# A transformer kernel's first stage on one core: the memory norm placed behind the third query block, weight residuals placed ahead of long VectorE pieces, tables and rotations spread

## What is computed

```python
mem_n = rms_norm(mem, mem_norm)                  # mem: 256 x 1024
h  = rms_norm(x, mix_norm[0])                    # x: 1024 x 1024
kv = mem_n @ w_mem_kv[l]                         # for both layers: memory keys and values
p  = h @ w_in                                    # 2048 columns
q, k, v, mq = split(p, [1024, 1280, 1536])
q, k = partial_rotary(q, positions), partial_rotary(k, positions)
attn = window_gqa(q, k, v, sinks)                # the next stage
```

## Time and profile before

| | us |
|---|---|
| median of 3 runs | 3354.19 (3350.89 to 3355.37) |
| the profiled execution, its own time | 3352.99 |
| span of its trace | 3351.2 |
| TensorE busy | 3127.3 (93%) |
| VectorE busy | 1694.6 (51%) |
| ScalarE busy | 1110.0 (33%) |
| the attention's first matmul starts at | 296.18 |

### The profile page before, as it was taken

One profiled execution on the slowest core, in us unless ns is written; L12 is line 12 of the kernel. 1 busy time (PEld: TensorE's weight loads), 2 busy tenths in 40 slices (PEclk: granted clock), 3 DMA queues, 4 the chain that ended last, 5 costly groups with the idle time before them and its releaser, 6 DMA issues.

```text
span 3351.2 us, 34636 instructions
## 1 busy us (share of the span) xinstructions
PE 3127.3 (93%) x14248; PEld 2414.6 (72%) x14258; DVE 1694.6 (51%) x2152; ACT 1110.0 (33%) x1726; POOL 130.6 (4%) x100
## 2 busy tenths in 40 slices
PE   7799989999999999999889999999998899997788
PEld 5686557788888888877667788888886686664556
DVE  6545864544444433599644533333335526664455
ACT  4213652311111111488532211111114417775332
POOL 0001530000000000000000000000002200000000
PEclk9899999999999999999899999999999899999889
DMA  3230011121222211211211111111111220001112
GB/s 135 85 95 26 1 57 38 38 82 63 76 70 75 69 51 51 82 41 41 84 55 38 51 44 50 45 47 48 46 49 57 79 91 20 19 26 69 32 45 101
DMA packets 54366, 190.44 MB, mean 57 GB/s; under 512 B 6272, under 2 KB 6656, under 8 KB 54080
## 3 DMA queue, kind: packets, MB, share of 16 engines
q1 hardware_dynamic: 54208, 188.22, 17.1%
HBM read 172.20 MB, written 14.68 MB: 56 GB/s over the span
## 4 chain that ended last, share of the span: by engine, by line
PE 73%; DVE 13%; ACT 10%; issue 3%; POOL 0%; DMA 0%; DVEq 0%; ACTq 0%; SPq 0%; POOLq 0%
PE PS L283 72%; ACT p L138 8%; DVE p L141 5%; DVE p L144 2%; DVE sm L499 1%; PE PS L534 1%; ACT wsp L138 1%; ACT H L138 1%; DVE p L148 1%; DVE p L1149 1%; DVE wsp L141 1%; DVE H L141 1%; ACT L138 1%; DVE p L547 0%; DVE p L149 0%
## 5 line engine op out<-in xcount | busy, mean ns | idle before, releaser
L283 PE MATMUL PS<-H,wsp 128*128 128x512 f32 x6864 | 1639.4, 399 | 107.6 <-DVE p L144 33.4
L283 PEld LDWEIGHTS PS<-H,wsp 128*128 128x128 f32 x6864 | 1309.8, 192 | 423.8 <-issue 58.0
L283 PE MATMUL PS<-p,wsp 128*128 128x512 f32 (+1 forms) x3840 | 895.1, 393 | 30.3 <-DVE p L141 20.7
L283 PEld LDWEIGHTS PS<-p,wsp 128*128 128x128 f32 x3840 | 713.8, 190 | 207.0 <-ACT wsp L138 21.5
L138 ACT ACTIVATE p<-p 128x1024 f32<-128x1024 f32 (+7 forms) x426 | 360.7, 871 | 879.9 <-DVE p L144 706.4
L138 ACT ACTIVATE wsp<-raw 128x1024 fp32r<-128x1024 f32 (+1 forms) x266 | 275.7, 1039 | 744.4 <-PE PS L283 576.7
L141 DVE TENSOR_TENSOR p<-p,PS 128x1024 f32<-128x1024 f32 (+2 forms) x232 | 244.3, 1053 | 498.2 <-PE PS L283 498.2
L141 DVE TENSOR_TENSOR wsp<-raw,wsp 128x1024 fp32r<-128x1024 f32 (+1 forms) x266 | 322.3, 1216 | 160.2 <-ACT wsp L138 154.9
L141 DVE TENSOR_TENSOR p<-PS,p 128x1024 f32<-128x1024 f32 (+1 forms) x114 | 130.7, 1148 | 443.5 <-PE PS L283 419.4
L283 PE MATMUL PS<-p 128*64 128x256 f32 (+9 forms) x1432 | 291.8, 472 | 23.9 <-ACT p L138 10.3
L141 DVE TENSOR_TENSOR p<-p 128x1024 fp32r<-128x1024 f32 (+6 forms) x245 | 243.4, 1000 | 110.0 <-ACT p L138 107.8
(11 more groups left out here) (71 smaller groups left out, 1167.9 us busy)
## 6 DMA issues: line engine op xcount, KB each, us to landing
raw<-in_in_dram SPq DMA_DIRECT2D x70, 512.0 KB, 3.6
raw<-in_dn_dram SPq DMA_DIRECT2D x68, 512.0 KB, 3.5
raw<-in_up_dram SPq DMA_DIRECT2D x64, 512.0 KB, 3.5
raw<-in_out_dram SPq DMA_DIRECT2D x40, 512.0 KB, 3.5
p<-in_ada_dram SPq DMA_DIRECT2D x24, 512.0 KB, 4.5
p<-in_x_dram SPq DMA_DIRECT2D x16, 512.0 KB, 7.5
raw<-in_kv_dram SPq DMA_DIRECT2D x16, 512.0 KB, 3.7
spill_dram<-p SPq DMA_DIRECT2D x16, 512.0 KB, 2.9
```

The lines of the kernel that those rows point to most:

```text
L283: return pe(lambda e: e.matmul(o, l, r, start=start, stop=stop, **kw), *a)
```

## The change

The order of the same work, nothing else:

- The list `order` has the query blocks and the memory blocks in another sequence: blocks 0 to 5 of `in0` first, and one query block between two pairs of memory blocks from then on.
- MR, the memory norm's factor, is made behind `q_block(2)` instead of before the first two evacuations. Its matmuls so take another place in the turn of PSUM pairs.
- `ahead()` is new: it calls `split` for the next three blocks at once, and it stands before each long VectorE piece.
- The tables: angles and cosine stand behind `q_block(3)` as before, the sine now behind `q_block(4)`.
- The rotations of two blocks stand behind the evacuation of the memory keys or values that come after them, with the splits ahead of them.
- `softplus()` stands behind the value rows and the last rotation.

```diff
--- before.py
+++ after.py
@@ -186,9 +186,9 @@
             for i in idx:
                 order.append((name, i, pieces))
 
-        blocks("in0", range(5))
-        for i, at_ in ((5, ("kv0", 0, 2)), (6, ("kv0", 2, 4)), (7, ("kv0", 4, 8)), (8, ("kv1", 0, 2)),
-                       (9, ("kv1", 2, 4)), (None, ("kv1", 4, 8))):
+        blocks("in0", range(6))
+        for i, at_ in ((6, ("kv0", 0, 2)), (7, ("kv0", 2, 4)), (8, ("kv0", 4, 8)), (9, ("kv1", 0, 2)),
+                       (None, ("kv1", 2, 8))):
             blocks(at_[0], range(*at_[1:]))
             if i:
                 blocks("in0", [i])
@@ -639,8 +639,6 @@
         at[0] = b0 + 2
         split(b0 + 2)
         box["r"] = finish(st, R, buf(84), buf(80), buf(92))
-        MR = buf(51, 256)
-        mr = finish(mst, MR, buf(52, 256), buf(53, 256), buf(54, 256), 256)
         for j, p in enumerate(pairs):
             fr = scaled(j, PS[:, 2 * p:2 * p + 2, :].rearrange("p a b -> p (a b)"), firsts[j])
             free[2 * p] = free[2 * p + 1] = fr
@@ -735,51 +733,46 @@
 
             project_rows(f"kv{l}", 4, 2, MHk, evv)
 
+        def ahead():
+            for x in range(LA + 1):
+                split(at[0] + x)
+
         q_block(2)
+        MR = buf(51, 256)
+        mr = finish(mst, MR, buf(52, 256), buf(53, 256), buf(54, 256), 256)
+        ahead()
         for k in range(8):
             mem_part(k)
         mends = [*MHops[7], *MHops[6], c_cb, c_tri]
         q_block(3)
+        ahead()
         angles()
         rope["cos"] = sine(Ct, 0.25)
+        q_block(4)
+        ahead()
         rope["sin"] = sine(St, 0.0)
-        q_block(4)
         rope["clear"] = [pool(lambda e, rt=rt: e.memset(rt, 0.0), rope["sin"]) for rt in rots]
-        softplus()
-        swap(0)
-        swap(1)
+        q_block(5)
         kv0, kv1 = [], []
-        mem_keys(0, MK, 0, kv0)
-        q_block(5)
         for n in (0, 1):
-            rotate(n)
-        for n in (2, 3):
             swap(n)
-        mem_keys(0, MK, 2, kv0)
-        q_block(6)
-        for n in (2, 3):
-            rotate(n)
-        for n in (4, 5):
-            swap(n)
-        mem_values(0, MV, kv0)
-        q_block(7)
-        for n in (4, 5):
-            rotate(n)
-        for n in (6, 7):
-            swap(n)
-        mem_keys(1, MK1, 0, kv1)
-        q_block(8)
-        for n in (6, 7):
-            rotate(n)
+        for i, more in enumerate((lambda: mem_keys(0, MK, 0, kv0), lambda: mem_keys(0, MK, 2, kv0),
+                                  lambda: mem_values(0, MV, kv0), lambda: mem_keys(1, MK1, 0, kv1))):
+            more()
+            ahead()
+            for n in (2 * i, 2 * i + 1):
+                rotate(n)
+            for n in (2 * i + 2, 2 * i + 3):
+                if n < 9:
+                    swap(n)
+            q_block(6 + i)
         mem_keys(1, MK1, 2, kv1)
-        swap(8)
-        q_block(9)
-        mem_values(1, MV1, kv1)
+        ahead()
         rotate(8)
         swap(9)
+        mem_values(1, MV1, kv1)
         mk_sp = [Q.dma(None, D["mk"], MK1[:, :, :], *kv1), Q.dma(None, D["mv"], MV1[:, :, :], *kv1)]
         kv_done = kv0 + kv1 + [Q.last("pe")]
-        lam_ready = lamd["ready"]
 
         def columns(R, r):
 
@@ -951,6 +944,8 @@
 
         project_rows("in0", 2, 8, Hk, rows_to(Vt, True, *kv_done))
         rotate(9)
+        softplus()
+        lam_ready = lamd["ready"]
 
         def by_R(T, R, r, *after):
             def ev(n, p, ps, op):
```

## The result

| | before | changed |
|---|---|---|
| median, us | 3354.32 (3350.89 to 3355.37, 4 runs) | 3299.97 (3299.63 to 3300.27, 4 runs) |
| ratio | | 0.984 (95% interval 0.9823 to 0.9857) |
| span of the profiled execution | 3351.2 | 3298.4 |
| start of the sums of squares of x | 33.24 | 34.02 |
| start of `columns` | 225.18 | 177.21 |

The kernel is 54.3 us faster where 49 were forecast (3305). Of the profiled executions' 52.8 us, 48.0 lie before the attention starts. The other 4.8 lie behind it, in stages whose code and order did not change.

A forecast was written before the change was run, and what follows sets the result against it. TensorE's first-stage waits and low clock, 54.8 us, bound the gain; summed terms put `columns` 49 us earlier, so 3353.0 - 49 = 3304, plus 1.2 for the median, 3305 us. Own range 3301 to 3309, 8-in-10 range 3299 to 3318.

The forecast's parts named there:

- What bounds the stage: First stage: TensorE's waits of 38.8 us and low clock of 16.0 us are the most the change can win.
- the two ways of adding up: Gain before `columns`: 49.0 us from summing the new timeline, or 49.8 from 54.8 less 5.0.
- The third query block: First gap, 11.46 us: block 2 gets the fourth PSUM pair and starts behind x's sums at about 36.8 us.
- VectorE's long pieces: Memory norm through tables: VectorE's queue leaves TensorE one wait, 3.0 us, before the query block behind the first keys.
- The low clock behind it: After the wait behind the first keys: TensorE's lowered clock costs 2.0 us.
- The rounds: Query block plus two key blocks, 16.8 us: covers at each step remove waits of 3.90, 4.01, 3.90 and 3.90 us.
- unknown landing L of a swap: In the rounds: time for a swap's 32 KB transfers to land, bounded by 0 and 19 us, taken as 3.
- tightest weight load behind a swap: SyncE, in the rounds: lands at E + 20.5, E being the keys' end, for a block split at E + 22 or later.
- Softplus costs nothing behind the value rows: Behind the value rows: 5.2 us of softplus fits VectorE's 13 us of work, its residual needed only 21.9 us in.
- The sum: End of the first stage: all terms put `columns` at 176.2 us instead of 225.18, 49.0 us earlier.
- The whole span moves: From `columns` on, order is unchanged, so the whole span moves by 49 us; over 4 us change behind refutes it.
- no low clock and no stall: Rival, 10%: at the first keys, faster tables or a short gap costing no clock give 3300 to 3302 us.

The follow-up runs named there:

- half-way run: Changed kernel with the memory norm's factor behind the first two evacuations but still ahead of the third query block: 3305.89 us.
- the repeat: The changed kernel run once more, unaltered: median 3300.44 us.
- the eleven rows of the table: Changed kernel, its variants, two repeats, and the kernel before with only the norm moved: medians from 3296.22 to 3340.18 us.

## Why the prediction was right, point by point

- *What bounds the stage, 54.8 us to be won.* Right. Four of the waits could be put back at will with their old lengths. The size was some 0.7 us too large: single undisturbed pieces of the kernel before took 11.09 us (a query block), 3.01 (half of two key blocks) and 5.76 (half of the values), more than the 10.93, 2.93 and 5.68 that I had subtracted. This is about the 0.8 us by which the two ways of adding up differ.
- *The third query block.* Right: it started at 37.05 directly behind the sums (36.8 forecast), block 3 without a wait. The half-way run shows that the PSUM pair is 8.66 of the 11.46 us.
- *VectorE's long pieces.* Right in the chain and in its size: 3.17 us of wait (3.0), the residual's copy behind the second Sin, and removing 3.4 us from the chain removes the wait. Softplus in this chain costs its full length, 6.0 us where I had 5.2 for it.
- *The low clock behind it, 2.0 us.* The mechanism was right, the size isn't fixed. Against the 11.07 us of the undisturbed blocks it was 2.8 us in the profiled execution, 0.1 in the repeat and in the run with the rotations moved, 1.7 with the added matmuls, and 2.6 behind the wait of 9.21 us with softplus back. So neither "2.0 us" nor "might cost nothing" is right for this kernel as such: each was nearly met in some executions.
- *The rounds.* Right: no wait in any. The unknown landing L of a swap was 1.7 us (four DMAs issued until 93.6, rotation at 95.30 behind a wait for the DMA), where I took 3 from a weight load. The 2.0 us of the Trainium skill (DMA: Bandwidth & Descriptors, section Anatomy of one DMA) came nearer, though the page fits them to DMAs issued from GpSimd, and these go out from SyncE. The tightest weight load behind a swap comes, by the terms given for it (9.6, 6.2 and 4.3), to E + 20.1 and not 20.5; the cover only grows by it. What I did not separate is that the rotations' place does this, and `ahead()` in the rounds nothing.
- *Softplus costs nothing behind the value rows.* Right: from `columns` to the attention it is 71.0 us in both kernels.
- *The sum, 49.0 for `columns`.* 48.0 measured (176.2 forecast, 177.21). From the start of the sums on it is 48.75; the other 0.8 us is that the sums began later in the changed kernel's execution, with nothing changed ahead of them.
- *"The whole span moves" by it.* This step failed. I held the part behind to be constant and set a bound of 4 us on it; it moved by 4.8. The runs show that it varies from 3048.0 to 3056.9 us with no change in it, through TensorE's granted clock, and twice for one kernel. The 5 us between 3305 and 3300 are of this size; the stage alone would have given 3306. So it is chance that 54.3 us look like nearly all of the 54.8, and that 3300 is where the rival "no low clock and no stall" had it (3300 to 3302): a wait of 3.17 us and a low clock of 2.8 us were both there. The kernel before seems to be at the long end: its medians in four sets of runs, less its traced start of the attention, are 3055.9 to 3058.1 us, those of the eleven rows of the table 3051.8 to 3055.6. Why, no run shows.

## What to carry to other kernels

Follow the queue of the engine that is waited for, instruction by instruction, in the new order and with the old durations; here it gave the waits of the changed kernel, with softplus back and with the rotations moved within 0.3 us, and missed the one without `ahead()` by 1.4, while subtracting waits from the total would have failed (7 us for 14, 10 for 14). A buffer taken in turn belongs to whoever is coded first, so a small early user can cost a large one its start. And when a change of some us is measured on a kernel of 3300, compare the stage that changed in two traces, from its own first instruction on, and not only the medians: the unchanged rest behind it moves by up to 9 us, and what lies ahead of it by up to 2.7.

## What the hardware showed beyond that

The same wait of TensorE, 3.17 us, was followed by a block of 11.14, 11.16, 12.75 or 13.89 us in four executions. An undisturbed one took 11.07, so a short wait cost 0.1 to 2.8 us more, differently from run to run. Longer waits did not cost more clock: 2.6 us behind 9.21, and 2.6 behind 11.46. Over the 3050 us behind the attention's start, where TensorE also stands still over a hundred times in the trace of the changed kernel, its busy time differs by 11 us between the shortest and the longest execution, for the same matmuls. That these 11 us are the sum of many such small differences is argued, not shown.
